# A hybrid streaming encoder step on one Trainium2 core: the first norm's scaling on ScalarE and its low parts on GpSimd, eight PSUM banks for the second projection, eight buffers for the output projections' weights

## What is computed

```python
# layer AB                                   # layer CD
p = rmsnorm(x, g) @ w_in                     p = rmsnorm(x, g) @ w_in
oa = chunk_band_attention(qa, ka, va)        oc = sliding_window_attention(qc, kc, vc, sinks)
ob = forget_attention(qb, kb, vb, logf)      score = sum_h wi_h * relu(qi_h . ki)       # indexer
mix = concat(oa*silu(ga), ob*silu(gb))       od = attention over the top-256 keys by score
x = x + mix @ w_out                          mix = concat(oc*silu(gc), od*silu(gd)); x = x + mix @ w_out
# and a final rmsnorm; k, v and logf of each layer are outputs too
```

## Time and profile before

| quantity | value |
|---|---|
| median of 3 runs (lowest, highest) | 4283.44 us (4275.76, 4285.5) |
| the profiled execution: its time, its span | 4278.92 us, 4277.1 us |
| busy PE, DVE, ACT, POOL | 3807.0, 2249.2, 1597.5, 681.5 us |
| mean granted PE clock | 0.950 |
| first norm | 0 to 96.58 us |
| mix1, from its start to block (1,0)'s transposes | 1944.11 to 1989.62 us |
| second projection: search, masks | 2522.8 to 2902.9, 2902.9 to 3063.5 us |
| mix2 up to the same point | 4015.24 to 4061.48 us |

### The profile page before, as it was taken

One profiled execution on the slowest core, in us unless ns is written; L12 is line 12 of the kernel. 1 busy time (PEld: TensorE's weight loads), 2 busy tenths in 40 slices (PEclk: granted clock), 3 DMA queues, 4 the chain that ended last, 5 costly groups with the idle time before them and its releaser, 6 DMA issues. The chain is left out here.

```text
span 4277.1 us, 51419 instructions
## 1 busy us (share of the span) xinstructions
PE 3807.0 (89%) x18129; PEld 2633.1 (62%) x18129; DVE 2249.2 (53%) x4858; ACT 1597.5 (37%) x2424; POOL 681.5 (16%) x408
## 2 busy tenths in 40 slices
PE   4999999978999999996989689899686799999698
PEld 3689988976776666665855544444254455555476
DVE  7211111128886544542310599998587877666332
ACT  3101100114544443433310489993254333333332
POOL 3100000002222111102410000000133432211143
PEclk9999999988999999998999899999898899999899
DMA  5222222234444233304421210111324111100243
GB/s 188 63 81 67 66 71 72 68 85 99 104 111 98 60 74 68 76 1 164 160 97 47 61 57 37 57 57 62 105 76 106 44 32 35 25 11 3 99 157 128
DMA packets 222512, 328.51 MB, mean 77 GB/s; under 512 B 22224, under 2 KB 129032, under 8 KB 220896
## 3 DMA queue, kind: packets, MB, share of 16 engines
q1 hardware_dynamic: 173280, 236.21, 19.3%
q10 hardware_dynamic: 43776, 72.50, 4.6%
q0 software_dynamic: 5216, 16.70, 1.8%
HBM read 214.35 MB, written 110.99 MB: 76 GB/s over the span
## 5 line engine op out<-in xcount | busy, mean ns | idle before, releaser
L1017 PE MATMUL attAB_p_o<-attAB_pt,attAB_v 128*65 128x512 f32 (+3 forms) x1120 | 432.7, 484 | 0.2 <-ACT attAB_pt L1064 0.2
L497 DVE COPY ab_stage<-ab_pA 128x256 f32<-128x256 f32 (+1 forms) x108 | 56.5, 523 | 600.3 <-PE ab_pA L466 565.9
L1104 DVE TENSOR_REDUCE attAB_mx<-attAB_p_s 128x1 f32<-128x512 f32 (+2 forms) x360 | 209.3, 608 | 285.1 <-PE attAB_p_s L952 174.9
L2360 DVE TENSOR_SCALAR_CACHE_REDUCE cd_junk<-score,cd_thr 128x512 bf16<-128x512 f32 (+8 forms) x288 | 350.4, 1275 | 1.4 <-DVE cd_thr L2377 0.3
L2398 ACT ACTIVATE cd_gate<-score,cd_thr 128x384 bf16<-128x384 f32 (+2 forms) x192 | 322.3, 1679 | 23.3 <-DVE cd_thr L2377 16.1
L994 PE MATMUL attAB_p_t<-attAB_q_a,attAB_k_a 128*128 128x512 f32 (+3 forms) x560 | 301.7, 543 | 17.4 <-DVE attAB_s_t L1148 15.6
L464 PE MATMUL ab_pA<-ab_W_hi,h_hi 128*128 128x256 f32 x1088 | 309.0, 284 | 3.2 <-PE ab_pA L466 3.1
L495 ACT ACTIVATE ab_stage<-ab_pA 128x256 f32<-128x256 f32 (+1 forms) x108 | 50.1, 464 | 697.1 <-PE ab_pA L466 666.8
L465 PE MATMUL ab_pA<-ab_W_lo,h_hi 128*128 128x256 f32 x1088 | 307.9, 283 | 0.0
L466 PE MATMUL ab_pA<-ab_W_hi,h_lo 128*128 128x256 f32 x1088 | 307.8, 283 | 0.0
L1625 PE MATMUL attD_p_o<-attD_pt,attD_v 128*65 128x512 f32 x548 | 287.5, 606 | 0.0
(11 more groups left out here) (343 smaller groups left out, 8778.3 us busy)
## 6 DMA issues: line engine op xcount, KB each, us to landing
attAB_raw<-t_k SPq DMA_DIRECT2D x32, 640.0 KB, 7.4
attAB_raw<-t_q SPq DMA_DIRECT2D x32, 640.0 KB, 9.8
t_qg<-cd_stage SPq DMA_DIRECT2D x74, 256.0 KB, 2.0
ab_W_raw<-in_w_ab SPq DMA_DIRECT2D x17, 1024.0 KB, 5.7
mix_o<-t_o SPq DMA_DIRECT2D x34, 512.0 KB, 4.4
t_q<-ab_stage ACTq DMA_DIRECT2D x40, 256.0 KB, 2.0
t_k<-ab_stage ACTq DMA_DIRECT2D x40, 256.0 KB, 2.0
norm_x<-in_x ACTq DMA_DIRECT2D x17, 512.0 KB, 3.7
```

Of the source, the lines that this page charges most:

```text
L1017: done = nc.tensor.matmul(p_o[u % 2][0:VW, i0 * P:(i0 + n) * P], left, pt[c % NPT][:, at * P:(at + n) * P], start=(c == plan.chunks_of[u][ ...
L2360: nc.vector.tensor_scalar(junk[nth % 2][:, 0:widths[n]], sc[n][:], T[:, n:n + 1], None, ALU.is_ge, ALU.add, accum_out=cnt[s % 2][:, n:n + ...
```

## The change

In the first norm ACT does the scaling of x in place of POOL, and POOL does the subtraction `leave` in place of DVE. ACT's order becomes square(b+1), scale(b), round(b-1); POOL's becomes root(b), leave(b-1). x gets a fourth buffer, the square's discarded output becomes bf16, and two small bias lines share one tile. In both mix stages the weights go to eight buffers (x0, x1, gate1, sig1, sq0, sq1, xn0, xn1), so that all eight loads are issued without a wait; block (0,1)'s row loads wait for the third split, its sigmoid for the fourth; ACT's and DVE's hi and lo parts of block (0,0) come ahead of weight tiles 6 and 7; PE multiplies half q = 0 of block (0,0) with one wait per weight tile, transposes block (0,1) after that half, and then multiplies q = 1. The second projection gets eight PSUM banks, LEAD 4 and PACE 0.56, and ACT copies only 128 columns of the narrow units.

```diff
@@ first_norm
-        NX = 3
+        NX = 4
-        sq = sb("sq", [P, D])
+        sq = sb("sq", [P, D], BF16)
...
+                def round_rows(b):
+                    act.wait_ge(kept, (b + 1) * G)
+                    nc.scalar.activation(h_hi[:, :, b * P:(b + 1) * P], h[b % 2][:], ACT.Copy).then_inc(rounded, 1)
                 square(0)
                 for b in range(NB):
                     if b + 1 < NB:
                         square(b + 1)
-                    act.wait_ge(kept, (b + 1) * G)
-                    nc.scalar.activation(h_hi[:, :, b * P:(b + 1) * P], h[b % 2][:], ACT.Copy).then_inc(rounded, 1)
-                    if b + NX < NB:
-                        load(b + NX)
+                    act.wait_ge(rooted, b + 1)
+                    act.wait_ge(squared, b + 1)
+                    nc.scalar.activation(x[b % NX][:], x[b % NX][:], ACT.Copy, scale=rstd[:, b:b + 1]).then_inc(scaled, 1)
+                    if b >= 1:
+                        round_rows(b - 1)
+                        if b - 1 + NX < NB:
+                            load(b - 1 + NX)
+                round_rows(NB - 1)
...
             def _(pool):
+                def leave(b):
+                    pool.wait_ge(rounded, b + 1)
+                    rows = slice(b * P, (b + 1) * P)
+                    nc.gpsimd.tensor_tensor(h_lo[:, :, rows], h[b % 2][:], h_hi[:, :, rows].bitcast(F32), ALU.subtract
+                                            ).then_inc(split, 1)
...
                 for b in range(NB):
-                    pool.wait_ge(varied, b + 1)
-                    nc.gpsimd.tensor_tensor(rstd[:, b:b + 1], var[:, b:b + 1], expo[:], ALU.pow).then_inc(rooted, 1)
-                    pool.wait_ge(rooted, b + 1)
-                    nc.gpsimd.tensor_tensor(x[b % NX][:], x[b % NX][:], rstd[:, b:b + 1].broadcast_to([P, D]), ALU.mult
-                                            ).then_inc(scaled, 1)
+                    if b >= 2:
+                        pool.wait_ge(split, b - 1)
+                    root(b)
+                    if b >= 1:
+                        pool.wait_ge(rooted, b + 1)
+                        leave(b - 1)
+                leave(NB - 1)
@@ mix_out
-        raw = sq + xn
+        raw = x + gt[1:] + sg[1:] + sq + xn
...
                     for k in range(KT):
-                        if k >= NRAW:
-                            sp.wait_ge(w_split, k - NRAW + 1)
                         sp.dma_start(raw[k % NRAW][:], w_dram[k * P:(k + 1) * P, :]).then_inc(w_in[k % NRAW], 16)
...
                         weights()
+                        sp.wait_ge(w_split, 3)
...
+                    if isinstance(n, int) and n == 0:
+                        sp.wait_ge(w_split, 1 + s)
                     sp.dma_start(x[s][:], x_dram[rows, :]).then_inc(x_in[s], 16)
...
+                    if isinstance(n, int) and n == 0 and s == 1:
+                        act.wait_ge(w_split, 4)
                     nc.scalar.activation(sg[s][:], gt[s][:], ACT.Sigmoid).then_inc(sig[s], 1)
...
+                        for k in range(KT):
+                            if k == KT - 2:
+                                round_mixed(0, 0)
...
+                def turn_mixed(n, s):
+                    if not (isinstance(n, int) and n == 0 and s == 1):
+                        lead(n, s)
...
-                    if is_first(n, s):
-                        pe.wait_ge(w_split, KT)
                     pe.wait_ge(m_kept[s], n * G + G)
                     pe.wait_ge(added[s], n * G)
                     for q in range(G):
+                        if is_first(n, s) and q == 1:
+                            lead(0, 1)
                         for k in range(KT):
+                            if is_first(n, s) and q == 0:
+                                pe.wait_ge(w_split, k + 1)
...
+                            if k == KT - 2:
+                                keep_mixed(0, 0)
                             dve.wait_ge(w_rounded, k + 1)
@@ project_cd
-        BANKS = 4
+        BANKS = 8
...
-        STEPS, LEAD, PACE, EARLY, TILES = 32, 2, 0.6, 4, 6
+        STEPS, LEAD, PACE, EARLY, TILES = 32, 4, 0.56, 4, 6
...
-                    nc.scalar.activation(stage[u % 2][:], pA[u % BANKS][:], ACT.Copy).then_inc(ev[u % BANKS], 1)
+                    w = ROWS - (RC - 1) * BANK if u < 2 * TUNITS and u % RC == RC - 1 else BANK
+                    nc.scalar.activation(stage[u % 2][:, 0:w], pA[u % BANKS][:, 0:w], ACT.Copy).then_inc(ev[u % BANKS], 1)
```

More of the change, by code:

```diff
@@ L122, in __init__ @@
         self.t5 = sb("t5", [2 * H, 32])
-        self.line_a = sb("line_a", [H, LA])
+        lines = sb("lines", [32 + 2 * H, LA])
+        self.line_a, self.line_d = lines[0:H, :], lines[32:32 + 2 * H, 0:LT]
         self.line_t = sb("line_t", [2 * H, LT])
-        self.line_d = sb("line_d", [2 * H, LT])
         self.flip = sb("flip", [P, P])
@@ L149, in move @@
         sp.wait_ge(self.lines, 2 + len(d.t5_runs))
-        sp.dma_start(d.line_a, self.line_a[:]).then_inc(self.stored, 16)
+        sp.dma_start(d.line_a, self.line_a).then_inc(self.stored, 16)
         sp.dma_start(d.line_t, self.line_t[:]).then_inc(self.stored, 16)
         sp.wait_ge(self.rel, 1)
-        sp.dma_start(d.line_d, self.line_d[:]).then_inc(self.stored, 16)
+        sp.dma_start(d.line_d, self.line_d).then_inc(self.stored, 16)
         sp.wait_ge(self.stored, 48)
@@ L188, in draw @@
         dve.wait_ge(self.lines, 2 + len(self.d.t5_runs))
-        nc.vector.tensor_scalar(self.line_d[:], line_t[:], t5[:, 15:16], None, ALU.subtract).then_inc(self.rel, 1)
+        nc.vector.tensor_scalar(self.line_d, line_t[:], t5[:, 15:16], None, ALU.subtract).then_inc(self.rel, 1)
     def keep(self, dve, n):
@@ L261, in _, with root @@
                         square(b + 1)
-                    act.wait_ge(kept, (b + 1) * G)
-                    nc.scalar.activation(h_hi[:, :, b * P:(b + 1) * P], h[b % 2][:], ACT.Copy).then_inc(rounded, 1)
-                    if b + NX < NB:
-                        load(b + NX)
+                    act.wait_ge(rooted, b + 1)
[6 more added lines that the diff above has]
+                round_rows(NB - 1)
             @block.gpsimd
             def _(pool):
+                def root(b):
+                    pool.wait_ge(varied, b + 1)
+                    nc.gpsimd.tensor_tensor(rstd[:, b:b + 1], var[:, b:b + 1], expo[:], ALU.pow).then_inc(rooted, 1)
+                def leave(b):
[3 more added lines that the diff above has]
+                                            ).then_inc(split, 1)
                 nc.gpsimd.memset(expo[:], -0.5).then_inc(fixed, 1)
@@ L299, in variance @@
                                             ).then_inc(varied, 1)
[L301 to L305, removed]
                 tiles.draw(dve)
@@ L321, in _ @@
                                                 ALU.mult).then_inc(kept, 1)
-                    if b >= 1:
-                        leave(b - 1)
                     for n in pieces_behind(b):
                         tiles.keep(dve, n)
-                leave(NB - 1)
 def group_units(kind):
@@ L1994, in sigmoid, with round_mixed @@
                     act.wait_ge(gated[s], n)
+                    if isinstance(n, int) and n == 0 and s == 1:
+                        act.wait_ge(w_split, 4)
                     nc.scalar.activation(sg[s][:], gt[s][:], ACT.Sigmoid).then_inc(sig[s], 1)
-                def lead(n, s):
-                    if is_first(n, s):
[L1999 to L2002, removed]
+                def round_mixed(n, s):
                     act.wait_ge(multiplied[s], n)
@@ L2008, in lead @@
                                              ).then_inc(m_rounded[s], 1)
+                def lead(n, s):
+                    if is_first(n, s):
+                        sigmoid(0, 0)
+                        for k in range(KT):
+                            if k == KT - 2:
+                                round_mixed(0, 0)
+                            act.wait_ge(w_in[k % NRAW], 16 * (k // NRAW + 1))
+                            nc.scalar.activation(W_hi[:, k, :], raw[k % NRAW][:], ACT.Copy).then_inc(w_rounded, 1)
+                    else:
+                        round_mixed(n, s)
                     if not is_last(n, s):
@@ L2095, in trail @@
                         turn_normed(*last_block(n, s))
-                in_turn(pe, lead, trail)
+                in_turn(pe, turn_mixed, trail)
                 if not final:
@@ L2101, in _, with keep_mixed @@
             def _(dve):
[L2102 to L2106, removed]
-                def lead(n, s):
+                def lead(n, s):
+                    if is_first(n, s):
+                        for k in range(KT):
+                            if k == KT - 2:
+                                keep_mixed(0, 0)
+                            dve.wait_ge(w_rounded, k + 1)
+                            nc.vector.tensor_tensor(W_lo[:, k, :], raw[k % NRAW][:], W_hi[:, k, :].bitcast(F32), ALU.subtract
```

(5 more changed lines are left out.)

1 line of the change is left out of this document (removed).

## The result

The changed kernel takes 4240.34 us (median of 4 runs, 4237.54 to 4244.76) against 4282.46 for the kernel before, measured beside it: a ratio of 0.9903 with a 95% interval of 0.9891 to 0.9914. The forecast was 4239. The profiled execution took 4237.54 us with a span of 4235.6, at a mean granted clock of 0.954 (before: 4278.92, 4277.1, 0.950).

What follows compares the result with a forecast made beforehand. PE bounds the long middle; the change touches four places where PE is not the limit. +5.3 - 28.5 - 18 = -41.2 us gives 4237.7 from the profiled execution, 4242.2 from the median; forecast between, 4239, range 4221 to 4264.

Steps and rivals of the forecast that it cites:

- a ring through root, scale, round and subtraction: First norm: ACT and POOL work one after the other, once round per block, 5.22 us; stage 5.3 us longer.
- The scale where the ring closes: First norm: the third scale on ACT, expected to start at 20.8 us.
- the slow subtraction (3.2 us): First norm, rival: POOL's subtraction takes 3.2 us, +14 over the sum, whole time 4253; chance 0.08.
- the slower case: First norm: a subtraction of 5.0 us or longer makes the kernel slower than before, 4290 at 5.5 us; chance 0.03.
- The rival in which the ring does not bind: First norm: ACT's work alone sets 3.4 us per block, stage ends near 79 us, whole time 4217; chance 0.05.
- 27.7 + 2 - 1: Second projection, us: 27.7 off DVE's gate waits, 2 saved in the search, 1 lost to copy pairs; given as -28.5.
- The 1 us for pairs of copies that wait for a stage buffer: Second projection: a loss of 1 us, taken off the gain.
- PE's work done ahead: Second projection: eight banks put PE up to eight units ahead at the search's end, not four; 28 us of work.
- PE's lower clock, the rival: Second projection: busy PE gets less clock, or weights come late; only some 8 of 28.5 us remain, 4259; chance 0.06.
- POOL's products of block (1,0) as the next to be late: Mix heads: after the change POOL's gate product of block (1,0), not PE, is what is late next.
- The half product: Mix heads: half of block (0,0)'s 12.6 us product on PE, 6.3 us, made 6.9 by slow first matmuls.
- 8.5 us: Mix heads: from block (0,1)'s transposes to the end of POOL's product for (1,0), against 7.9 us needed by PE.

Runs made afterwards that it cites:

- e5_banks8: Kernel before with eight banks and narrow copies in the second projection, old placing of copies (LEAD 2, PACE 0.6): 4252.74 us, ratio 0.9931.
- e6_pace: Kernel before with only LEAD 4 and PACE 0.56 in the second projection, still four banks: 4282.72 us, ratio 1.0001.

## Why the prediction was right

**First norm: +5.3 predicted, +5.9 measured.** The step that counted, that the written order closes a ring through root, scale, round and subtraction, is shown: opening it takes 20 to 23 us off the stage, and one more subtraction in it costs 41.4. Its terms came out at 0.58, 1.06, 1.18 and 2.43 start to start, 5.25 against 5.22. The scale where the ring closes started at 21.22, not 20.8, which with 14 times 0.03 makes 0.8; 0.6 of it reached the next stage (102.53, not 101.9). Of the rivals, the slow subtraction (3.2 us) is refuted by 2.35, and with it the slower case, which wanted 5.0. The rival in which the ring does not bind had the right price: 79 us and 4217 were what it gave, and 79.4 and 82.7 us, 4218 and 4223, are what the kernel with the open ring took; its condition alone was not met. That price was met in part by luck: the period was 3.10 us and not 3.4, and waits that it did not count made up for it (7.9 us for x in the 79.4).

The Trainium skill, "Perfetto Trace Analysis", section "Optimizing Scalar/DVE Operations", says that work moved between GpSimd and VectorE might not gain, because they share a port. Where POOL's order is right the traces agree that nothing much is gained: the first norm takes 79.4 and 82.7 us with the subtraction on POOL and 82.5 us with it on DVE. But the port is not what held those two kernels: the subtractions took 2.34 to 2.40 us on POOL and 1.21 to 1.23 on DVE, none lengthened by the other engine.

**Second projection: -28.5 predicted, -29.1 measured.** The prediction's terms, 27.7 + 2 - 1, add up to 28.7 and not 28.5. DVE's waits for the gate were to fall by 27.7 and fell by 27.1; the search was to save 2 and took 378.2 us from its first count to its last threshold in place of 380.3. With the old placing, narrow copies (and eight banks) shorten the search by 1.1 us, to 379.2 (e5_banks8); the new placing alone makes it 0.3 us longer (e6_pace); the rest of the 2.1 needs both. The 1 us for pairs of copies that wait for a stage buffer shows as 4.0 us of ACT's waits for a store against 1.7 before; that any of it reached the masks is not shown. PE was to end about 3024, which the gains of earlier stages (predicted +5 - 9) put at 3020: it ended at 3021.7. The reason given, PE's work done ahead, is shown by e5_banks8 for the banks. Its size was put too high and another term at nothing: at the last threshold PE had 280 matmuls left instead of 330, which is 3.1 units of 16 ahead and not 4, 23.0 us of work and not 28. The other 5.8 us came from its wait for a copy behind the search, 8.03 us before and 2.20 now. That the two make up 28.8 is luck. PE's lower clock, the rival, is refuted: 0.98 granted in the mask part (0.96 before), and the gain is whole.

**Mix heads: -9 each predicted, -10.0 and -9.2 measured.** Counted from each stage's start, the first product was expected at 20.8 and came at 20.5; block (0,1)'s sigmoid at 21.4 to 22.9 and came at 21.7; block (1,0)'s transposes at 35.9 to 37.4, and they came at 36.1 and 37.05. The prediction had POOL's products of block (1,0) as the next to be late, and the last timeline row of mix1 above names them. Two terms of the reasoning were off, and that they cancelled is luck. The half product was to take 6.9 us and took 7.9, so that it and not POOL decided block (0,1)'s transposes: these came straight behind it, at 28.4 us, 0.7 us after POOL had finished their rows (1980.34). From there to the end of POOL's product for (1,0) the prediction had 8.5 us, read from the kernel before, in which those transposes took 1.97 us; now they took 1.04, and the way 7.7. Of mix1's 10.0 us this head gives 9.4; the other 0.6 is within the spread of the stage.

## What to carry to other kernels

Before moving an instruction to an idle engine, write the new order of every queue and follow it around: if engine A's item waits for B's and B's stands behind one that waits for A's, the sum of all of them is the period, however idle each engine is, and one move of a small instruction ahead of a long one can be worth more than the offload (21 us here against at most 3 for the offload itself, 79.4 and 82.7 us against 82.5). Where two engines hand over units through banks, count how many finished units stand ready when the consumer changes its pace: about three more of 7 us each, and a shorter stop behind them, took 27 us from the waits of a third engine that never touches them.

## What the hardware showed beyond what was expected

**The rows fit DVE and POOL taking turns and not sharing.** In the head of mix1 (timeline above) POOL's first product ends at 1962.96. Two DVE splits, issued from 1961.84 on, take 5.49 us in place of 2.35 for later pairs, and POOL's second product 3.21 in place of 2.40. Suppose that neither runs beside the other. Then the first split starts at 1962.96 and takes some 1.2 us, to 1964.2; POOL's second product follows for 2.35, to 1966.5 (measured end 1966.25); and the second split, for 1.1, to 1967.4 (from the measured end) or 1967.6 (measured 1967.33). POOL's first product, which was running when the split was issued, was not lengthened: 2.35 us. In the first norm before, the subtraction issued at 61.13 should by the same count run from the end of POOL's product, 62.61, for 1.1 to 1.2 us, to 63.8; it ended at 63.69. POOL's products there took 1.892 to 1.896 us, all seventeen. The Trainium skill, "SBUF — State Buffer", section "SBUF: two separate sides", states this rule, an exclusive hold for a whole instruction between a DVE instruction with two SBUF inputs and a GpSimd one that reads SBUF, and the rows agree with it. In the new first norm DVE has no such instruction left, and POOL's subtractions took 2.34 to 2.37 us throughout. That the two take turns was not tried by an experiment of its own.

**Two engines at full load in lock step.** In the kernel with the open ring, between 53 and 60 us, neither POOL (0.63 + 2.47 from start to start) nor ACT (scale 1.06, round 0.95, square with its sum 1.10) has idle time: both come to 3.10 us. An ACT block was expected at 3.4, from durations; start to start scale and round are about 0.1 us shorter than their rows.
